# Hybrid decoder layer: normed tiles transposed by DMA, a sixth FFN weight slot, alternating state products

## What is computed

```python
h = layer_norm(concat([meta, x]), ln_emb_g, ln_emb_b)
proj = h @ w_in                                   # 4864 columns
hq, hf, hi, hg, aq, ak, av, gates = split(proj)
y_hg  = hgrn2_mixer(hq, hf, hi, hg, ...) @ w_branch_hg       # gated linear recurrence, 4 heads of 128
y_att = swa_sink_attention(aq, ak, av, sinks) @ w_branch_attn # window 128, 8 heads, 2 KV heads
g_hg, g_att = split(sigmoid(gates))
mix = (g_hg * y_hg + g_att * y_att) @ w_out
h = layer_norm(ALPHA * h + mix, ln1_g, ln1_b)
a, u = split(h @ w_ffn_in)                        # 2 x 2816 columns
h = layer_norm(ALPHA * h + (silu(a) * u) @ w_ffn_out, ln2_g, ln2_b)
return h[:, BLOCK:]                               # the meta positions are dropped
```

## Time and profile before

| | us |
|---|---|
| time before, median of 3 runs (lowest and highest) | 3982.31 (3821.74 to 4189.14) |
| the profiled execution, its own time | 3823.93 |
| its span on the slowest core | 3822.3 |
| spans of the eight cores | 3798.1 to 3822.3 |
| mean granted TensorE clock, all cores | 0.987 to 0.988 of full |

### The profile page before, as it was taken

How to read it: one execution, slowest core, us unless ns; L and a number is a source line. 1 busy time by engine, 2 the same in 40 slices (tenths; PEclk the granted TensorE clock), 3 DMA queues, 4 the chain that set the end, 5 groups by cost and what they waited for, 6 DMA issues and landing times.

```text
span 3822.3 us, 68943 instructions; the slowest of 8 cores (3798.1 to 3822.3 us)
## 1 busy us (share of the span) xinstructions
PE 3643.3 (95%) x20673; PEld 1752.9 (46%) x20673; DVE 2449.6 (64%) x4577; ACT 1484.6 (39%) x2649; POOL 523.8 (14%) x615
## 2 busy tenths in 40 slices
PE   5789899999999999999999999999999999999997
PEld 2344344444544444444444444444444444444443
DVE  5565575576756667666666767657675666766643
ACT  4344252533525344342534425353352534425310
POOL 3212221111101011110111101011110101111000
PEclk9899999999999999999999999999999999999998
DMA  8978887766665576655666666576665667665564
GB/s 178 205 212 168 204 224 189 217 186 221 185 191 187 177 225 191 219 176 174 209 189 223 184 202 191 167 218 187 221 192 175 195 188 223 185 215 169 154 197 129
DMA packets 335910, 739.87 MB, mean 194 GB/s; under 512 B 37680, under 2 KB 46128, under 8 KB 335552
## 3 DMA queue, kind: packets, MB, share of 16 engines
q1 hardware_dynamic: 314816, 695.35, 58.4%
q0 software_dynamic: 20736, 40.12, 7.3%
HBM read 647.50 MB, written 127.93 MB: 203 GB/s over the span
## 4 chain that ended last, share of the span: by engine, by line
PE 82%; DMA 9%; DVE 2%; issue 2%; POOL 1%; SPq 1%; ACT 1%; another core or an unknown queue 1%; DVEq 0%; POOLq 0%; ACTq 0%
PE ps L1251 29%; PE ps L675 18%; PE ps L1282 12%; PE ps L1226 6%; PE ps L1198 5%; DMA XT<-x 3%; PE ps L883 3%; PE ps L795 3%; PE ps L588 2%; DMA W<-wi_b 1%; PE ps L834 1%; DMA gT<-w_f 1%; POOL rs L575 1%; DMA W<-wi_f 1%; SPq L519 1%
## 5 line engine op out<-in xcount | busy, mean ns | idle before, releaser
L1251 PE MATMUL ps<-h1T,W 128*128 128x512 bf16 x5560 | 1260.8, 380 | 18.3 <-DMA W<-wi_b 9.6
L1251 PEld LDWEIGHTS ps<-h1T,W 128*128 128x128 bf16 x5560 | 528.4, 98 | 643.2 <-issue 43.7
L675 PE MATMUL ps<-hT,W 128*128 128x512 bf16 x3424 | 793.0, 380 | 4.8 <-DMA W<-w_b 3.9
L1282 PE MATMUL ps<-W,gT 128*128 128x512 bf16 x2816 | 640.5, 380 | 12.5 <-DMA W<-wd_f 7.4
L575 POOL TENSOR_TENSOR rs<-ve,cneg 128x1 f32<-128x1 f32 x193 | 264.0, 1368 | 2156.4 <-DVE ve L573 2156.2
L681 ACT ACTIVATE th<-ps 128x512 bf16<-128x512 f32 x448 | 264.6, 597 | 670.7 <-PE ps L675 665.0
L675 PEld LDWEIGHTS ps<-hT,W 128*128 128x128 bf16 x3424 | 331.6, 98 | 402.5 <-issue 15.3
L681 ACT ACTIVATE thf<-ps 128x512 bf16<-128x512 f32 x352 | 210.1, 597 | 709.4 <-PE ps L1251 690.3
L1258 DVE SCALAR_TENSOR_TENSOR s<-thf,ps 128x512 f32<-128x512 bf16 x352 | 241.5, 686 | 282.7 <-ACT thf L681 246.2
L1282 PEld LDWEIGHTS ps<-W,gT 128*128 128x128 bf16 x2816 | 269.1, 98 | 319.0 <-issue 22.2
L1261 DVE TENSOR_TENSOR gT<-s,ps 128x512 bf16<-128x512 f32 x352 | 241.0, 685 | 88.7 <-PE ps L1251 79.7
(11 more groups left out here) (184 smaller groups left out, 4074.8 us busy)
## 6 DMA issues: line engine op xcount, KB each, us to landing
W<-wi_b SPq DMA_DIRECT2D x638, 256.0 KB, 3.0
W<-w_b SPq DMA_DIRECT2D x540, 256.0 KB, 2.9
W<-wd_b SPq DMA_DIRECT2D x319, 256.0 KB, 4.5
h_scr<-XT SPq DMA_DIRECT2D x120, 512.0 KB, 4.8
WB<-wt_b SPq DMA_DIRECT2D x75, 512.0 KB, 6.5
y_out<-FR SPq DMA_DIRECT2D x64, 512.0 KB, 4.8
XT<-x SPq DMA_DIRECT2D x60, 512.0 KB, 6.8
XT<-h_scr SPq DMA_DIRECT2D x60, 512.0 KB, 5.5
```

The costliest lines, as they stand in the source:

```text
L675: inst = e.matmul(P(bank), wt[:, c * 128:(c + 1) * 128], hT[:, c, :], start=(c == 0), stop=(c == 7))
L1251: inst = e.matmul(P(bk), w[0][:, c * 128:(c + 1) * 128], h1T[:, c, :], start=(c == 0), stop=(c == 7))
L1282: inst = e.matmul(P(bks[i]), gT[:, j, i * 128:(i + 1) * 128], w[0][:, jj * 512:(jj + 1) * 512], start=(j == 0), stop=(j == NJ - 1))
```

## The change

Four things.

- The tiles of every group but the first are transposed by DMA. `to_hT` gets `xbar`: after ACT's cast it issues one transposing DMA from ACT's queue, `hb` to `hT` or `h1T`, in place of TensorE's transposes and ACT's copy. Each of the eight tiles of a group has its own `hb`, laid over the eight slots of `R12`.
- The room of the old `hb` goes to a sixth slot of `W2`.
- `recur` issues the eight products of a tile in one call that alternates between the two halves of 64 rows and fills two banks; before there were two calls, one per half.
- In group 0 the weight loads wait for the load of x tile 1 or 3 (`xin`) and no longer for its layer norm. The constants of the due times and of the scheduler are changed.

```diff
-PERIOD = 226.0
+PERIOD = 214.472
-PF_REL = 140.0
-W_LEAD = 12.0
-WB_LEAD = 20.0
-P1_LEAD = 100.0
-A2_LO = 0.72
-PB_LO = 0.92
-A1_DVE = 1.0
-F_LO = 0.0
-F_HI = 1.15
-F_VLEAD = 200.0
+PF_REL = 172.392
+M_REL = 0.0
+W_LEAD = 9.212
+WB_LEAD = 24.057
+XB_BYTES = 262144
+P1_LEAD = 125
+A2_LO = 0.705
+PB_LO = 0.93
+A1_DVE = 1.116
+F_LO = 0.096
+F_HI = 1.267
+F_VLEAD = 126.204
...
-SEM_LAG = 0.12
-DMA_RATE = 320e3
-DMA_LAG = 2.2
-SP_LAG = 0.5
-POW_T = 1.2
-PE_LAG = 0.3
+SEM_LAG = 0.166
+DMA_RATE = 293453.479
+DMA_LAG = 2.802
+SP_LAG = 0.366
+POW_T = 1.283
+PE_LAG = 0.652
...
-        W2 = ring("W2", 5, [128, 1024], BF16)
+        W2 = ring("W2", 6, [128, 1024], BF16)
...
-        hb = ring("hb", 1, [128, D], BF16)
+        hb = [(R12[:, i, :].bitcast(BF16), BR[i]) for i in range(8)]
...
             wload(ap, [b], "w1_%d" % k, w1_f[i], w1_b[i], ("w1", i), 262144, 2 if first else 0,
-                  after=[FR[1 if i < 4 else 3][1]] if first else [])
+                  after=[xin[1 if i < 4 else 3]] if first else [])
...
-                  after=[FR[3][1]] if first and name == "wt" else [] if first else chain)
+                  after=[xin[3]] if first and name == "wt" else [] if first else chain)
...
+        xin = [Buf("xin%d" % i) for i in range(4)]
...
-            op("sp", lambda e: e.dma_start(out=xt[:], in_=x[t * 128:(t + 1) * 128, :]), SP_T, writes=[Bx] + old,
+            op("sp", lambda e: e.dma_start(out=xt[:], in_=x[t * 128:(t + 1) * 128, :]), SP_T, writes=[Bx] + old + xin[t:t + 1],
...
-        def to_hT(src, Bsrc, hbt, dst_fn, Bdst, n=128):
+        def to_hT(src, Bsrc, hbt, dst_fn, Bdst, n=128, xbar=None):
             hbx, Bhb = hbt
             op("act", lambda e: e.copy(out=hbx[0:n, :], in_=src), actc(1024), reads=Bsrc, writes=[Bhb])
+            if xbar:
+                op("act", lambda e: e.dma_start_transpose(out=dst_fn(), in_=hbx), 0.1, reads=[Bhb], writes=Bdst,
+                   dma=xbar, nbytes=XB_BYTES)
+                return
             bk = Bank("tr")
...
-                to_hT(xt[:], [Bx], hb[0], (lambda i=i: hT[:, :, i * 128:(i + 1) * 128]), [BhT[i]])
+                to_hT(xt[:], [Bx], hb[i], (lambda i=i: hT[:, :, i * 128:(i + 1) * 128]), [BhT[i]],
+                      xbar="xb%d" % i if g > 0 else None)
...
+            bus = [Bank("U0"), Bank("U1")]
+
+            def fu(e):
+                inst = None
+                for h in range(4):
+                    for ch in range(2):
+                        rows = slice(ch * 64, ch * 64 + 64)
+                        inst = e.matmul(P(bus[ch])[:, h * 128:(h + 1) * 128], kbk[rows, h, i * 128:(i + 1) * 128],
+                                        vbf[rows, i, h * 128:(h + 1) * 128], start=True, stop=True)
+                return inst
+            op("pe", fu, mmc(128, 4) + 0.1, reads=Bkbk + [Bvb[i]], writes=bus)
             for ch in range(2):
-                bu = Bank("U")
-                rows = slice(ch * 64, ch * 64 + 64)
-
-                def fu(e, bu=bu, rows=rows):
-                    inst = None
-                    for h in range(4):
-                        inst = e.matmul(P(bu)[:, h * 128:(h + 1) * 128], kbk[rows, h, i * 128:(i + 1) * 128],
-                                        vbf[rows, i, h * 128:(h + 1) * 128], start=True, stop=True)
-                    return inst
-                op("pe", fu, mmc(128, 4), reads=Bkbk + [Bvb[i]], writes=[bu])
+                bu = bus[ch]
...
-                to_hT(rx[:], [Br], hb[0], (lambda i=i: h1T[:, :, i * 128:(i + 1) * 128]),
-                      [Bh1T[i]] + ([z[1] for z in hs] if g == 0 else []))
+                to_hT(rx[:], [Br], hb[4 + i], (lambda i=i: h1T[:, :, i * 128:(i + 1) * 128]),
+                      [Bh1T[i]] + ([z[1] for z in hs] if g == 0 else []),
+                      xbar="xc%d" % i if g > 0 else None)
```

More of the change, by code:

```diff
@@ L556, in wbload, with layer_norm @@
                   "wb_%d" % slot, src_f[i], src_b[i], (name, i), 524288, 2 if first else 0, lead=WB_LEAD,
-                  after=[FR[3][1]] if first and name == "wt" else [] if first else chain)
+                  after=[xin[3]] if first and name == "wt" else [] if first else chain)
             wb_last[:] = [BWB[2 * slot]]
-        def layer_norm(k, src, Bs, gi, eps, pp=128):
+        def layer_norm(k, src, Bs, gi, eps, pp=128, rel=0.0):
             i = counters.get("ln%d" % k, 0)
@@ L569, in f @@
                 return e.bn_stats(out=st6[0:pp, 1, :], in_=src[:, 512:1024])
-            op("dve", f, 1.28, reads=Bs, writes=[Bst])
+            op("dve", f, 1.28, reads=Bs, writes=[Bst], rel=rel)
             op("dve", lambda e: e.bn_aggr(out=mv[0:pp], in_=st6[0:pp].rearrange("p a b -> p (a b)")), 0.2, reads=[Bst],
@@ L661, in to_hT @@
                actc(8 * n), reads=[bk], writes=Bdst)
-        layer_norm(0, mt, Bmt, 0, EPS, 16)
-        to_hT(mt, Bmt, hb[0], lambda: hTm[:], [BhTm], 16)
+        layer_norm(0, mt, Bmt, 0, EPS, 16, M_REL)
+        to_hT(mt, Bmt, hb[7], lambda: hTm[:], [BhTm], 16)
         P1TOT = 124.0
```

## The result

The kernel after takes 1.0514 times as long as the one before, with an interval of 1.0406 to 1.0622. Its profiled execution took 4057.0 us, that of before 3823.9. The forecast was 3732, within 3695 to 3860, so it missed in direction and in size.

A forecast was written before the change was run, and what follows sets the result against it. TensorE, busy 3643.3 of 3822.3 us, was taken as the bound. Sum: 3822.3 - 54.0 + 15 - 23.3 - 4.7 - 13 - 7 - 5 = 3730.3 of span, plus 1.6: 3732 us, range 3695 to 3860.

The forecast's parts named there:

- cost that at nothing: ACT's queue: a transpose issue of 0.9 us blocks tanh evictions no longer than today's 1.01 us copy, so no cost.
- The landing: Transposing DMA from issue to data in hT or h1T: taken as 5 us, between 2.9 and 10.1.
- The late hT: First projection matmuls of groups 1 to 15: hT about 1 us late per group, +15 us (0 to +90).
- Transposes off TensorE: Groups 1 to 15: 120 tiles at 0.45 us each leave TensorE, -54.0 us.
- Waits of the transpose line: TensorE's waits at its transposes for hb's cast, FR and statistics after the start go, -23.3 us (at least 12.0).
- priorities and slot: Reordering trims unnamed standing time, 5 us (-10 to 15); sixth slot cuts waits on wi and wd loads, 7 us (0 to 15).
- State products: recur: one alternating call in place of two lets apart-standing halves run together, -4.7 us (bounds 0 and 6).
- The start: Group 0: weight loads start 14 us earlier, less a bit for POOL's rsqrt order, -13 us (0 to 20).
- C: Rival: transposes served one after another, TensorE stands still above 4.5 us apiece; some 3890 us at 5.9 each; chance 0.15.
- B: Rival: hT lands 3 to 8 us late per group, nothing more; 3762 to 3837 us, gain given back; chance 0.20.
- D: Rival: the start doesn't move, POOL's queue still holds the loads behind the rsqrt steps; 3745 us; chance 0.07.

The follow-up runs named there:

- e19: e18 plus 12 copies by ACT of each group's fourth h1T tile into a spare tile that nothing reads; 3902 us, 1.025 against before.
- e18: The kernel after with its transposes on SP's queue and five W2 slots in place of six; 3801 us.
- m1: Small separate program: ACT issues DMA transposes singly and four in a row, beside SP loads of varied packet size, up to twelve under way; alone 3.1 us.
- e6: The kernel after with all 120 transposes issued from SP's queue in place of ACT's; 3740 us, 0.9839 against before.
- e9: The kernel after, on ACT's queue, each transpose waiting for the landing of the one before, planner told; 1.0598 against before.
- e15: e9 with its chained transposes on SP's queue in place of ACT's; 3849 to 3914 us on cores 0 to 3.
- e1: The kernel after with every tile transposed by TensorE and copied by ACT as before, all else kept; 0.9954 against before.
- e12: e6 with the planner told 1.3 us of SP and 2.2 us of DMA engines per transpose; 3743 us, 0.9813 against before.
- e7: The kernel after without the transposing DMAs and with the old constants; 1.0028 against before.
- m2: Small separate program: DMA transposes from ACT's or SP's queue beside at most four SP loads; from ACT 7.4 and 11.7 us, from SP 5.6 and 6.3.
- e2: The kernel before with only the transposing DMAs from ACT's queue, old constants, five slots; 4200 us against 3822.
- e14: The kernel before with only the 120 transposing DMAs, from SP's queue, old constants, five slots; 1.0243 against before, 3902 us.

## Why the prediction was wrong, step by step

*The step that failed* is the price of a transposing DMA from ACT's queue, in both its terms. I put its issue at 0.9 us by SP's row of two loads, let it stand against the copy of 1.01 us that it replaces, and so "cost that at nothing". It measured 1.25 us alone and 3.1 in the mean (371 / 120), because an issue waits while transposes before it are under way. The text named the consequence ("If the issue took several us, banks would come back late") and gave it neither a price nor a chance. It was half of the case or more: TensorE waits 9.4 us per group for ACT's held copies (93.3 of 2400 us), and copies that hold ACT for a similar time cost 7.8 us per group by e19 against e18. The landing, put at 5 us by the rows of ordinary loads, measured 14.1 and 9.1. Those rows are of large packets in the queue that all the others use, and the transpose is small packets in a second one, which take turns with the large ones (m1). The late hT, +15 in the sum, measured some 43 (25.2 in the first 1000 us, 17.6 in the even stretch): too small, but not what turned the sign.

Of the 20.5 us per group between after (242.5) and e6 (222.0), 13.9 are standing time: 9.4 behind ACT's copies, 3.5 for wi loads, 1.8 for hT, less the 1.0 that e6 stands still. The other 6.6 are work at a lower clock. The experiments give some 8 for the hold (e19) and some 10 for the second queue without a hold (e9 against e15), by kernels that differ in more than that. Whether the two may be added isn't shown.

*Transposes off TensorE, -54.* Right: 960 instructions gone, and at full clock TensorE is busy 224.3 us per group in e1 (core 6) and 221.0 in e6, 3.3 less where 8 x 0.45 = 3.6 were counted. The page of after shows more busy time than before, not 55 to 60 us less, since its clock is lower.

*Waits of the transpose line, -23.3, priorities and slot, -12 together.* In e12 TensorE's waits in the even stretch are under 14 us in all. The waits for the cast of hb went; 7.6 of what is left are transposes of the attention (L590 on qr). The slot was mis-sized in a way that I had not seen: nothing with transposes on TensorE (e7: 1.003), 60 us with them on SP's queue.

*State products, -4.7.* 25.6 us busy for the 512 matmuls, before 32.3: 6.7, over the 4.7 taken and just over the bound of 6.

```profile
L1107 PE MATMUL ps<-vbf,kbk 64*128 64x128 bf16 x512 | 25.6, 220 | 0.1
```

*The start, -13.* The first weight load is issued at 15.72, before 28.15, and the DMA share from 20 to 30 us is 1.05 in place of 0.05:

```profile
15.72 2.29 POOL L518 DMA_DIRECT2D W<-w_f  x4 [8.46 <-DMA FR<-x]
```

```profile
20.00:30.00 10.00, 1.01 (x8) 0.77 (x8) 7.66 (x13) 2.63 (x5) 9.43 (x17) 1.00 1.05 165
```

The FFN of the first group begins 13 us earlier, at 205, not 218. The early loads alone don't do it: in e7, with its first load at 16.4 and the old constants, the FFN begins at 225. So the size was met, and that the loads are its cause isn't shown.

*The whole sum.* I gave 3732 us and 223 to 224 per group. With the transposes on SP's queue the same change takes 3740 to 3744, and 222.0. The sum comes out for a kernel in which the transposes share the queue of the loads. Its terms do so only in part: the slot is worth 60 us there and not 7, and the constants far more than 5.

*The rivals.* C had the sign and about the time (3890 and up), by another mechanism: it said that transposes are served one after another at over 5.9 us each. Without traffic four land 1.2 to 1.4 us apart; beside 2 KB packets a row of four took 26.5 us to land (80.2 to 106.7 in m1), 6.6 each, so there C's price is met. Its path is not: in the even stretch of after the median landings of a group's eight don't grow but are 11.1, 10.6, 8.7 and 3.6 us for h1T and 3.2, 14.9, 19.3 and 8.0 for hT, and what TensorE waits for is ACT's queue far more than hT. That C's time fits is luck. The Trainium skill's 1309 ns per 128x128 block (VectorE: DVE Perf Modes, The three transpose paths) would be an estimated 10.5 us for the eight blocks of a tile; m1 measured 3.1 for all eight alone. B was right in that hT lands late (25.2 us in the first 1000 us of after, then some 1.8 per group), less than its 3 to 8, and it left out the hold. D is out, as the start moved. The Trainium skill's other rule (Advanced Engine Details and Errata, X-Bar Transpose (TRN2)), transposes as fast as ordinary DMAs, agrees with m1 without traffic and in the queue of the loads, and not beside them in a queue of its own: 12.6 and 17.9 us.

*Open.* How many transposes a queue takes before it holds its engine, what the first 4 us of a transpose beside loads are, the cost of the chain in e9 and e15, and the 36 us that the tail of after takes longer were not settled. What the slot and the new constants give with SP's queue was measured together with the new order that each makes.

## What to carry to other kernels

Before a DMA is put on a compute engine's queue, ask what its issue costs when earlier ones are still under way, and what stands behind it on that engine: a copy out of PSUM or a cast behind a held issue stops TensorE, and the clock makes the stop dearer. Here the DMA of small packets belonged in the queue that carries the large ones beside it, and the slots that this queue fills had to allow for it. The engine whose wait is longest need not show the cause: the same held queue showed as late copies in one kernel and as late landings in another, and only the timeline of ACT told it. If a price that no row shows could reverse the sign, it is worth a chance and a time of its own in the forecast, not a sentence.

## What the runs showed of the hardware

- A DMA transpose of a 128x1024 bf16 tile is 1056 packets, 1024 of 256 B and 32 of 4 B (the 126720 of after). It lands in 3.1 us alone, 3.8 beside another queue's 512 B packets, 12.6 beside 2 KB and 17.9 beside 4 KB (m1, twelve loads on their way), and 5.6 and 6.3 in the queue of the loads itself (m2, four on their way).
- Packets of two queues take turns on the DMA engines, some 1.1 packets of the loads for each of the transpose, at 2 KB and at 4 KB alike (m1).
- Its issue takes 1.25 us on ACT or SP, and up to 11.8 us in m1 (core 1) and 18 in after when transposes of the same queue are under way beside large packets. 120 issues hold ACT for 371 us (after) and SP for 337 (e6).
- It slows its neighbours: with the constants of before wd loads land in 5.9 us (e2) and 5.6 (e14), in before in 4.5.
- After TensorE stood still for 5 to 10 us the granted clock fell to 0.87 and 0.67 of the stretch, and eight matmuls took 3.57 us for 1.89.
